# Up products of the feed-forward with the weights stationary and no turns afterwards

## The reference

```python
def rmsnorm(x, g):
    y = xf * lax.rsqrt(jnp.mean(xf * xf, axis=-1, keepdims=True) + EPS)
    return (y * g.astype(F32)).astype(x.dtype)

def conv_ffn(h, w_up, conv_w, conv_b, w_down):
    u = h @ w_up
    up = jnp.pad(u, ((0, 0), (1, 1), (0, 0)))
    u = sum(up[:, i:i + t] * conv_w[i] for i in range(3)) + conv_b
    a, g = jnp.split(u, 2, axis=-1)
    return (a * jax.nn.silu(g)) @ w_down

for layer in range(2):
    x = x + hybrid_mixer(rmsnorm(x, ln1_g[layer]), ...)
    x = x + conv_ffn(rmsnorm(x, ln2_g[layer]), w_up[layer], ...)
```

## Time and profile before

| | |
|---|---|
| time, median of 3 runs (lowest to highest) | 3482.24 us (3479.25 to 3486.41) |
| span of the profiled execution | 3481.7 us |
| busy PE / DVE / ACT | 3407.4 / 2272.8 / 1838.5 us |
| feed-forward of layer 0 / layer 1, by the first and last `w_up` load and what follows | from 1491 us on / up to the end of the span |
| `WL` by DVE (L1902) | 1056 x 1231 ns |
| `WH` by ACT (L1330) | 1056 x 1056 ns |

### The profile page before, as it was taken

How to read it: one execution, slowest core, us unless ns; L and a number is a source line. 1 busy time by engine, 2 the same in 40 slices (tenths; PEclk the granted TensorE clock), 3 DMA queues, 4 the chain that set the end, 5 groups by cost and what they waited for, 6 DMA issues and landing times.

```text
span 3481.7 us, 41485 instructions
## 1 busy us (share of the span) xinstructions
PE 3407.4 (98%) x16098; PEld 2758.3 (79%) x16098; DVE 2272.8 (65%) x3048; ACT 1838.5 (53%) x2505; POOL 161.9 (5%) x243
## 2 busy tenths in 40 slices
PE   8999999999999999999999999999999999999998
PEld 6878688777688867788888888888677888888887
DVE  5886665895665566566666666755665666766666
ACT  4555645646554366555544444543665555445545
POOL 3032000050000000000000000000000000000000
PEclk9999999999999999999999999999999999999999
DMA  7544355554365444456556556554444665565564
GB/s 204 166 143 138 103 173 162 170 148 127 106 201 151 125 146 133 169 178 192 188 181 193 188 180 195 185 163 120 154 136 163 194 188 188 184 192 185 179 198 156
DMA packets 399891, 578.50 MB, mean 166 GB/s; under 512 B 25505, under 2 KB 222617, under 8 KB 399312
## 3 DMA queue, kind: packets, MB, share of 16 engines
q1 hardware_dynamic: 393344, 557.94, 52.3%
q0 software_dynamic: 5904, 16.75, 1.6%
q10 hardware_dynamic: 448, 1.18, 0.1%
HBM read 570.78 MB, written 4.98 MB: 165 GB/s over the span
## 4 chain that ended last, share of the span: by engine, by line
PE 87%; ACT 4%; DVE 3%; POOL 3%; issue 2%; DMA 1%; ACTq 0%; DVEq 0%
PE PS L713 84%; PE PS L710 3%; POOL ZA L2618 1%; POOL SM L2615 1%; DVE WL L1902 1%; ACT WH L1330 1%; DMA RAW<-in_w_in 0%; DMA base_scratch<-ZA 0%; ACT AR L1706 0%; DMA lt_scratch<-AR 0%; ACT ZA L1411 0%; DMA AR<-base_scratch 0%; DMA ZA<-lt_scratch 0%; DMA AR<-in_b_conv_w 0%; DVE SM L2310 0%
## 5 line engine op out<-in xcount | busy, mean ns | idle before, releaser
L1902 DVE TENSOR_TENSOR WL<-RAW,WH 128x1024 fp32r<-128x1024 f32 x1056 | 1295.3, 1231 | 953.5 <-ACT WH L1330 950.7
L1330 ACT ACTIVATE WH<-RAW 128x1024 fp32r<-128x1024 f32 x1056 | 1106.9, 1056 | 1059.7 <-PE PS L713 689.6
L713 PE MATMUL PS<-WH,Ah 128*128 128x512 f32 x3520 | 1418.3, 403 | 19.0 <-DVE Al L1960 4.9
L713 PE MATMUL PS<-WL,Ah 128*128 128x512 f32 x3520 | 1377.3, 391 | 0.0
L713 PE MATMUL PS<-WH,Al 128*128 128x512 f32 x3520 | 1375.5, 391 | 0.0
L713 PEld LDWEIGHTS PS<-WH,Ah 128*128 128x128 f32 x3520 | 663.8, 189 | 187.4 <-issue 30.2
L713 PEld LDWEIGHTS PS<-WL,Ah 128*128 128x128 f32 x3520 | 663.1, 188 | 142.4
L713 PEld LDWEIGHTS PS<-WH,Al 128*128 128x128 f32 x3520 | 664.6, 189 | 136.4 <-issue 6.7
L713 PE MATMUL PS<-WH,Zh 128*128 128x512 f32 x704 | 278.3, 395 | 0.6
L713 PE MATMUL PS<-WH,Zl 128*128 128x512 f32 x704 | 274.2, 390 | 0.0
L713 PE MATMUL PS<-WL,Zh 128*128 128x512 f32 x704 | 274.2, 389 | 0.0
(11 more groups left out here) (324 smaller groups left out, 2121.0 us busy)
## 6 DMA issues: line engine op xcount, KB each, us to landing
RAW<-in_w_in SPq DMA_DIRECT2D x368, 512.0 KB, 3.7
RAW<-in_w_up SPq DMA_DIRECT2D x704, 256.0 KB, 3.1
RAW<-in_w_down SPq DMA_DIRECT2D x176, 512.0 KB, 3.9
RAW<-in_w_out SPq DMA_DIRECT2D x64, 512.0 KB, 3.6
RAW<-in_w_o SPq DMA_DIRECT2D x64, 512.0 KB, 3.7
RAW<-in_w_in SPq DMA_DIRECT2D x64, 256.0 KB, 3.1
AR<-in_c POOLq DMA_DIRECT2D x2, 1600.0 KB, 7.9
AR<-bias_scratch POOLq DMA_DIRECT2D x16, 192.0 KB, 4.0
```

The source lines that it names most:

```text
L713: return T.matmul(o, lhs, rhs, start=start, stop=stop, skip_group_check=True)
L1330: act(WH[:, j % NW, 0:n], raw_view(j), ACT.Copy).then_inc(*w_hi())
L1902: tt(WL[:, j % NW, 0:w], raw_view(j), WH[:, j % NW, 0:w].bitcast(F32), SUB).then_inc(*w_lo())
```

## The change

The up products alone are turned round. The high and the low activations of a k tile stand side by side in one buffer `AHL` (`Ah` and `Al` are now views of it). For each of the four blocks of 128 weight columns, `WH` is stationary and `[high | low]` moves as 512 columns, then `WL` is stationary and the high part moves as 256 columns, added to the first half of the bank. A chunk takes four banks, features on the partitions, and no turn is needed. ACT copies the low x high halves of the four banks to `UT` (1024 elements a partition), DVE adds the other halves, then multiplies by the tokens' 1/rms, which PE and DVE lay out along the free axis once a layer (`ROWS`). The taps read `UT` instead of PSUM. Up chunks alternate between banks 0 to 3 and 4 to 7; the down chunks of a group use all eight. In the diff the three pieces of `leave_up` stand in the order PE, ACT, DVE.

```diff
-        Ah = sb("Ah", [128, 16, 256], F32R)
-        Al = sb("Al", [128, 16, 256], F32R)
+        AHL = sb("AHL", [128, 16, 2, 256], F32R)
+        Ah, Al = AHL[:, :, 0, :], AHL[:, :, 1, :]
...
+        def banks_of(ch):
+
+            if ch.phase == "up":
+                return [4 * (ch.name % 2) + b for b in R4]
+            s = ch.index % 2
+            if ch.phase == "dn" and ch.name[0] < 10:
+                s = ch.name[1]
+            return [2 * s, 2 * s + 1]
...
+                    if ch.phase == "up":
+                        for b in R4:
+                            at = slice(128 * b, 128 * b + 128)
+                            if beg and ch.after[b]:
+                                T.wait_ge(*set_free(ch.after[b]))
+                            mm(PS[:, b0 + b, 0:512], wh[:, k, at], flat(AHL[:, kk, :, :]), beg, False)
+                            ins = mm(PS[:, b0 + b, 0:256], wl[:, k, at], hi[:, kk, :], False, end)
+                        continue
...
+                if c == 3 and r in (3, 5):
+                    T.wait_ge(*p_rs.at(2 * r + 1))
+                    T.wait_ge(*p_gt.at(gt_index(r, 2, 1)))
+                    for t in R2:
+                        ins = mm(PS[:, 4, 128 * t:128 * t + 128], RSTD[:, t:t + 1].broadcast_to([128, 128]), ident)
...
             def leave_up(ch):
-                for i in R4:
-                    for t in R2:
-                        o = 256 * (i % 2) + 128 * t
-                        ins = tr(PS[:, 4 + 2 * u + i // 2, o:o + 128], UT[u][:, t, 128 * i:128 * i + 128])
-                ins.then_inc(*f_pe(f"{l}.{c}.tr"))
...
+                A.wait_ge(*w_used.at(ch.end))
                 if c >= 2:
-                    A.wait_ge(*f_pe.at(f"{l}.{c - 2}.tr"))
-                scaled(UT[u], ch, f_act, [k + ".sc0", k + ".sc1"])
-                yield
-                yield
-                A.wait_ge(*f_pe.at(k + ".tr"))
+                    A.wait_ge(*f_dve.at(f"{l}.{c - 2}.b3"))
+                act(UT[u], PS[:, ch.banks[0]:ch.banks[0] + 4, 256:512], ACT.Copy).then_inc(*f_act(k + ".cp"))
+                yield
+                A.wait_ge(*f_dve.at(k + ".row"))
...
-                yield
+                V.wait_ge(*f_act.at(k + ".cp"))
+                tt(UT[u], PS[:, b0:b0 + 4, 0:256], UT[u], ADD).then_inc(*f_dve(k + ".sum"))
+                V.wait_ge(*f_dve.at(k + ".sum"))
+                tt(UT[u], UT[u], ROWS.unsqueeze(1).broadcast_to([128, 4, 256]), MUL).then_inc(*f_dve(k + ".row"))
                 yield
...
-                    stt(CV[u][:, i, 1:256], ps[:, 0:255], P(("fcw", l), q), CV[u][:, i, 1:256],
+                    stt(CV[u][:, i, 1:256], UT[u][:, i, 0:255], P(("fcw", l), q), CV[u][:, i, 1:256],
```

More of the change, by code:

```diff
@@ L504, in program @@
         ups = range(22)
-        f_act = steps("up_act", [f"{l}.{c}.{n}" for l in LL for c in ups for n in ("sc0", "sc1", "ct0", "ct1", "ct2", "ct3", "th", "hi")])
-        f_pe = steps("up_pe", [f"{l}.{c}.tr" for l in LL for c in ups])
+        f_act = steps("up_act", [f"{l}.{c}.{n}" for l in LL for c in ups for n in ("cp", "ct0", "ct1", "ct2", "ct3", "th", "hi")])
+        f_pe = steps("up_pe", [f"{l}.rows" for l in LL])
+        f_rows = steps("up_rows", [f"{l}.rows" for l in LL])
         f_dve = steps("up_dve", [f"{l}.{c}.{n}" for l in LL for c in ups
-                                 for n in ("a0", "a1", "a2", "a3", "b0", "b1", "b2", "b3", "th", "zz", "lo")])
+                                 for n in ("sum", "row", "a0", "a1", "a2", "a3", "b0", "b1", "b2", "b3", "th", "zz", "lo")])
         QW, KW, SK, ALG, DTB, LAMP, RDL = [], [], [], [], [], [], []
@@ L635, in program @@
         TH = [ar(8192, 2, 256), ar(8704, 2, 256)]
-        UT = [ar(9216, 2, 512), ar(10240, 2, 512)]
+        UT = [ar(9216, 4, 256), ar(10240, 4, 256)]
+        ROWS = ar(16640, 256)
         FG, XN = ar(4096, D), ar(0, 2, D)
@@ L654, in set_free @@
             if ch.phase == "up":
-                return f_act.at(f"{l}.{n}.sc1")
+                return f_dve.at(f"{l}.{n}.sum")
             if n in ("ba", "ga"):
@@ L668, in set_free @@
             return e_act.at(f"{l}.{n}." + ("cp" if n == "uba" else "th")) if n in ("uba", "ubg") else e_dve.at(f"{l}.{n}.g")
+        def banks_of(ch):
[5 more added lines that the diff above has]
+            return [2 * s, 2 * s + 1]
+        last_in = {}
+        for ch in in_order:
+            ch.banks = banks_of(ch)
+            ch.after = [last_in.get(b) for b in ch.banks]
+            last_in.update({b: ch for b in ch.banks})
         def merged_at(tag, l, k):
@@ L716, in tile @@
                 j, k0 = ch.tiles[n]
-                s, w, kp = ch.index % 2, ch.width, ch.kp
-                if n == 0 and ch.index >= 2:
-                    T.wait_ge(*set_free(in_order[ch.index - 2]))
+                w, kp = ch.width, ch.kp
+                b0 = ch.banks[0]
+                if n == 0 and ch.phase != "up" and ch.after[0]:
+                    T.wait_ge(*set_free(ch.after[0]))
+                if n == 0 and ch.phase == "up" and ch.name == 1:
+                    T.wait_ge(*p_gt.at(gt_index(3 + 2 * ch.l, 3, 1)))
+                    T.wait_ge(*f_rows.at(f"{ch.l}.rows"))
                 if needs(ch, n):
@@ L1910, in add_x @@
                     V.wait_ge(*x_added.at(added[0] - 4))
[L1911 to L1912 removed]
+                b0 = ch.banks[0]
+                tt(xs, PS[:, b0:b0 + 2, :], xs, ADD).then_inc(*x_added())
                 added[0] += 1
@@ L1960, in prepare @@
                     tt(Al[:, k0:k0 + 2, :], GT[:, k0:k0 + 2, :], Ah[:, k0:k0 + 2, :].bitcast(F32), SUB).then_inc(*p_lo())
+                if c == 3 and r in (3, 5):
+                    V.wait_ge(*f_pe.at(f"{(r - 3) // 2}.rows"))
+                    cp(ROWS, bank(4, 256)).then_inc(*f_rows(f"{(r - 3) // 2}.rows"))
                 e.flags.add(f"h{r}{c}")
@@ L2543, in leave_up @@
                 k = f"{l}.{c}"
-                yield
+                b0 = ch.banks[0]
+                V.wait_ge(*f_act.at(k + ".cp"))
+                if c == 0:
+                    V.wait_ge(*f_rows.at(f"{l}.rows"))
+                tt(UT[u], PS[:, b0:b0 + 4, 0:256], UT[u], ADD).then_inc(*f_dve(k + ".sum"))
+                V.wait_ge(*f_dve.at(k + ".sum"))
+                tt(UT[u], UT[u], ROWS.unsqueeze(1).broadcast_to([128, 4, 256]), MUL).then_inc(*f_dve(k + ".row"))
                 yield
```

17 lines of the change are left out of this document (6 added, 11 removed).

## The result

| | before | after |
|---|---|---|
| time, median (lowest to highest) | 3480.74 us (3478.20 to 3486.41) | 3559.68 us (3555.78 to 3560.22) |
| span of the profiled execution, granted clock | 3481.7 us, 0.995 | 3558.4 us, 0.988 |
| busy PE / DVE / ACT | 3407.4 / 2272.8 / 1838.5 us | 3433.3 / 2375.0 / 1836.1 us |

The changed kernel is slower: 1.0224 of the time before, with an interval of 1.021 to 1.0238. I had said slower by 0.5% with a range up to 3540 us; the time lies 20 us above that range. The profiled spans differ by 76.7 us, and these have to be found.

The account below looks back on a forecast made before the run. PE's own work, without gaps in the feed-forward, was taken as the bound. To the 3481.7 us span: turns -38.3, load waits -6.0, start +3.0, stalls +59.8, together +18.5; with 0.5 for the median, 3501 us, range 3468 to 3540.

Parts of the forecast that it names:

- the products: PE's up matmuls: cost the same, 1.363 us a k tile against 1.364, if 128-column loads hide behind 256 moving columns.
- The doubt: PE's weight loads: one load shows 189 ns, though loads overlap, so it might not hide behind 256 columns.
- rival B: Up products on PE: loads bind at 0.189 us each, adding 105 us, 3556 us in all; chance 0.09.
- rival A: Feed-forward: clock falls in the new stalls, 1.7 us each, 34 more if all odd ones fall, 3535 us; chance 0.16.
- odd stall: PE before the sixth tile after an odd up chunk: `WL` 1.97 us late, 1.70 shown idle.
- The stalls: PE waits for DVE's late `WL` before the sixth tile after each up chunk: 59.8 us in all.
- Even chunks: Behind even up chunks, without an add in DVE's queue, `WL` is 0.85 us late for the sixth tile.
- No turns: PE is rid of the turns of 44 up chunks, 0.87 us each: 38.3 us saved.
- Loads no longer wait for adds: Fourth down chunks: 20 waits of PE's loads for adds to x vanish, 0.3 us each, 6.0 us saved.
- The first chunk of layer 0: Start of layer 0's feed-forward: PE waits for DVE's add of the mixer's last output chunk, losing 1.64 us.
- start: First up chunk of each layer: PE's waits for banks plus four small matmuls for `ROWS`, 3.0 us more.
- Rival C: ACT and DVE behind up chunks: shorter chain, `WL` in time, faster from 0.42 us a chunk, e.g. 3463 us; chance 0.18.

Follow-up runs that it names:

- run 4: Changed kernel with each 512-column up matmul cut into two of 256, so all are 256 wide: 3571.64 us (one run).
- run 1: Changed kernel with one more yield on ACT and DVE, so the taps come one tile later: 3476.62 us, 0.9982 of before.
- run 5: Changed kernel with loads of 32 columns for low weights, high weights or both (three runs): 3554.11, 3556.42 and 3535.49 us.
- run 3: Changed kernel with the low weights also multiplying the low activations, so all up matmuls are 512 columns wide: 3799.75 us (one run).
- run 7: Changed kernel with taps one tile later and each tile's eight 512-column products ahead of its eight 256-column ones: 3467.36 us, 0.995 of before.
- run 2: Changed kernel with the taps one tile later behind odd up chunks alone: 3499.44 us, 1.004 of before.

## Why the prediction was wrong

**Where it failed: the products.** "So the products cost the same, provided that a load of 128 columns hides behind 256 moving ones" is the step. I put the term at 0; it measured +37 us, 0.105 on each of 352 tiles. The turns had shown a load every 0.109 us, and from this I concluded that 0.1136 was enough. But the turns move 128 columns each; the proviso was about loads beside moving operands of other widths, and no row of before showed that: rows 3 had loads of 32 columns. In the pairs the 256-column slots are 0.117 and, more than that, the 512-column slots beside them 0.235; only among themselves do the 256s with full loads take 0.120 (run 4). The doubt was raised, and the only price given to it was rival B's 0.189 a load, 105 us; the truth, a few per cent, lay between the two ends and was in neither case.

**The second half of the miss: rival A happened.** I gave it 0.16, because an odd stall would show 1.70 idle and the two rows of before put the edge between 1.82 and 1.99. The stalls show 1.88 to 2.24, as the chain is some 0.2 longer than worked out: the middle taps take 2.09 (1.92 assumed), and what stands ahead of them begins 0.02 to 0.05 later. Its price of 1.7 us a fall was right; 15 falls are 25.5 us. The edge itself was not one: it rested on one idle time of each kind, and behind the same 1.82 that had left the clock at 1.00 before, the clock of the changed kernel fell (PE, and the stretch that follows):

```profile
84.27 0.73 PE L730 MATMUL PS<-WH,AHL 128*128 128x512 f32 x2 [1.82 <-ACT ZA L1501]
```

```profile
85.00:90.00 5.00, 5.00 (x15) 3.05 (x14) 0.47 (x1) 1.03 (x2) 0.00 (x0) 0.66 0.42 129
```

Either term alone, added to the forecast, would have stayed within the range, 3501 + 37 = 3538 or 3501 + 25.5 = 3527; together they left it.

**The stalls were right in place and cause, and in their sum partly by luck.** Even chunks: 0.53 lost (0.85 forecast; the five longer up tiles ahead put the due time 5 x 0.105 back, so 0.85 + 0.2 - 0.53 = 0.52). Odd: 2.18 (1.97 forecast; down tiles stand behind them and are no longer than before). With 1.4 behind the third chunk of each layer, forecast at 0.85 like the other even ones and not explained by these runs: 2 x (11 x 0.53 + 1.4 + 10 x 2.18) = 58 us, or 60 with 2.00 shown, the mean of the 20 odd gaps, in place of 1.91; 59.8 was forecast. The longer chain and the longer tiles, neither of them foreseen, cancelled each other in this sum.

**What held besides.** No turns: -38.3. Loads no longer wait for adds (one of 0.9 is left, at a layer's start): -6.0 assumed. The first chunk of layer 0 waits 1.41 shown for the add of the mixer's last chunk; with the 0.16 by which a matmul runs past its slot, and the 0.07 by which the first slot is longer, that is the 1.64 forecast. The row of the changed kernel:

```profile
1505.41 0.47 PE L730 MATMUL PS<-AHL,WH 128*128 128x512 f32 x1 [1.41 <-DVE X L1937]
```

**The sum as measured.** The feed-forwards are marked off by starts of DVE's adds to x: the last one ahead of each, and each one's own last. Before, behind the 1505.36 of the earlier trace rows: the end of layer 0's feed-forward, the end of the second mixer, the end of layer 1's feed-forward.

```profile
2250.91 1.22 DVE L1912 TENSOR_TENSOR X<-PS,X 128x1024 f32<-128x1024 f32 x1
...
2726.82 1.23 DVE L1912 TENSOR_TENSOR X<-PS,X 128x1024 f32<-128x1024 f32 x1 [0.34 <-PE PS L713]
...
3469.19 1.23 DVE L1912 TENSOR_TENSOR X<-PS,X 128x1024 f32<-128x1024 f32 x1 [2.34 <-PE PS L713]
```

The same four in the changed kernel:

```profile
1504.04 1.22 DVE L1937 TENSOR_TENSOR X<-PS,X 128x1024 f32<-128x1024 f32 x1 [0.34 <-PE PS L730]
...
2289.89 1.22 DVE L1937 TENSOR_TENSOR X<-PS,X 128x1024 f32<-128x1024 f32 x1
...
2765.79 1.22 DVE L1937 TENSOR_TENSOR X<-PS,X 128x1024 f32<-128x1024 f32 x1 [0.34 <-PE PS L730]
...
3545.87 1.23 DVE L1937 TENSOR_TENSOR X<-PS,X 128x1024 f32<-128x1024 f32 x1 [2.89 <-PE PS L730]
```

The feed-forwards take 785.85 and 780.08 us instead of 745.55 and 742.37, 78.0 more. All else is 1.3 less, nearly all of it ahead of layer 0's feed-forward, where the products are those of before; the second mixer takes 475.90 against 475.91, although one fall of the clock lies in it now and none before. The terms for the feed-forwards: products +37, turns -38.3, waits -6.0, start +3.0, stalls +58 to 60, falls of the clock +25.5, together +79 to 81, against 78.0. In run 1, without stalls and falls, the feed-forwards take 743.42 and 739.40, 5.1 less than before, where the other four terms give -4.3. So the sum closes to within 1 to 3 us; no run separated the turns from the waits of the loads.

**Rival C** (a shorter chain) did not come, as the chain was longer. Its point of decision, 0.42 us a chunk, rested on products at 0 too: with them at +37 the change is worth 5 us in the feed-forwards even without any stall, and run 1 is 0.2% faster than before. **Rival B's** mechanism did not appear: the slots of 256 columns with full loads are 0.117 to 0.120 us, not the 0.189 that one load shows. That its 3556 us lies near the 3559.68 measured is chance. The Trainium skill's "Perfetto Trace Analysis" (Identifying the Most-Contended Engine) wants the busy share of the weight loads looked at. It is 79% in both kernels, though the size of the loads bears on the slots of the changed one (run 5).

## What to carry to other kernels

Work that is off the critical path still has a due time. List, for each engine that feeds the bottleneck, what stands ahead of the next thing it delivers, and shift the new work until the delivery is in time; here one `yield` on two engines was worth 83 us. A slot measured at one pair of load and moving widths is no price for another pair. Alternating widths cost more than the two alone (0.353 against 0.341 a pair), so keep matmuls of one width together; here this gave back 11 of the 37 us. When a forecast stall lies near the idle time after which the clock fell in the same trace, price the fall in with an even chance at least: the chain need be only 0.2 us longer, and the same 1.82 us of idle time was followed by no fall in one trace and by a fall in the other.

## What the runs showed of the hardware that was not expected

- A matmul of 256 columns takes 0.1136 us with loads of 32 columns, 0.120 with loads of 128 (run 4), and 0.117 in turn with 512s (changed kernel).
- A matmul of 512 columns takes 0.227 beside its like (run 3) and about 0.235 in turn with 256-column ones. In groups of eight between groups of these (run 7) the first five take 0.232 and the last three 0.227.
- Making one of a pair's two loads small gives 0.02 us a tile, making both gives 0.08 (run 5). Why stays open.
- In the feed-forwards the clock fell after 15 of 20 gaps of 1.88 to 2.24 us shown, and after none of 0.2 to 1.3 (changed kernel and run 2). Within that range the length does not decide: of two gaps of 1.91 in one layer (1756.45 and 1827.78) only the first was followed by a fall, and one of 2.24 (3372.85) kept 1.00.
- Nor is there an edge outside them: 1.82 (84.27) was followed by a fall where the same idle time before was not, and in the second mixer one of 1.10 (2489.95), by 0.66 in the stretch from 2490 to 2495. What decides stays open.
